# A hybrid decoder step on one core: weight loads held behind the row stores and the first gather, the decode rows turned later, and from expert 4 on the down product ahead of the next up products

## The reference, cut to what matters

```python
h  = x + merged @ w_o                        # 520 x 1024, w_o 1024 x 1024
hn = rmsnorm(h, norm2)
# hier_moe: top-1 of 4 groups, then top-2 of its 8 experts; 32 experts in all
ys = (silu(xb @ w1[e]) * (xb @ w3[e])) @ w2[e]     # w1, w3: 1024 x 512; w2: 512 x 1024
h  = h + sum over the two chosen experts of gate * ys
y  = rmsnorm(h, norm_f)
```

## Time and profile before

| | us |
|---|---|
| median of 3 runs | 1240.52 |
| the runs | 1240.52, 1242.89, 1231.26 |
| the profiled execution, its own time | 1231.87 |
| its span, first to last instruction | 1230.2 |
| PE busy in the span | 1077.6 (88%) |
| DVE, ACT, POOL busy | 348.9, 208.3, 136.8 |

### The profile page before, as it was taken

How to read it: one execution, slowest core, us unless ns; L and a number is a source line. 1 busy time by engine, 2 the same in 40 slices (tenths; PEclk the granted TensorE clock), 3 DMA queues, 4 the chain that set the end, 5 groups by cost and what they waited for, 6 DMA issues and landing times.

```text
span 1230.2 us, 16554 instructions
## 1 busy us (share of the span) xinstructions
PE 1077.6 (88%) x6863; PEld 777.5 (63%) x6863; DVE 348.9 (28%) x755; ACT 208.3 (17%) x410; POOL 136.8 (11%) x153
## 2 busy tenths in 40 slices
PE   7999999999999999999989659987787888887881
PEld 6888888888888878877845435544444444444440
DVE  4994107922322323222533411100000000000002
ACT  4103022144222222320022200000000000000002
POOL 2015300011000000000000011111111111111111
PEclk9999999999999999999999869989999999899896
DMA  6671851335465482198064568999999999999964
GB/s 220 248 264 38 296 213 50 121 99 190 180 245 213 163 330 68 35 366 336 1 258 189 213 235 329 415 412 420 416 421 419 419 419 420 422 420 416 419 276 149
DMA packets 45801, 330.96 MB, mean 269 GB/s; under 512 B 9144, under 2 KB 12296, under 8 KB 31648
## 3 DMA queue, kind: packets, MB, share of 16 engines
q1 hardware_dynamic: 31888, 258.57, 52.4%
q0 software_dynamic: 12112, 64.52, 15.0%
q10 hardware_dynamic: 1728, 6.84, 1.4%
HBM read 319.77 MB, written 62.37 MB: 311 GB/s over the span
## 4 chain that ended last, share of the span: by engine, by line
PE 63%; DMA 30%; ACT 3%; DVE 2%; issue 1%; ACTq 1%; SPq 0%; POOLq 0%; DVEq 0%
DMA arena<-in_w 25%; PE bank L822 13%; PE bank L647 13%; PE bank L1124 9%; PE bank L1006 5%; PE bank L1149 5%; PE bank L997 3%; DMA arena<-in_w_stream 2%; PE bank L660 1%; DMA hn_dram<-arena 1%; PE bank L737 1%; PE bank L918 1%; PE bank L811 1%; PE bank L837 1%; PE bank L858 1%
## 5 line engine op out<-in xcount | busy, mean ns | idle before, releaser
L1124 PE MATMUL bank<-arena 128*64 128x256 f32 x2048 | 267.3, 419 | 74.8 <-DMA arena<-in_w 71.2
L1124 PEld LDWEIGHTS bank<-arena 128*64 128x64 f32 x2048 | 164.2, 146 | 169.0 <-issue 59.6
L822 PE MATMUL bank<-arena 128*128 128x260 f32 x768 | 173.1, 384 | 0.0
L647 PE MATMUL bank<-arena 128*128 128x260 f32 x768 | 169.4, 383 | 0.7 <-DMA arena<-in_w_stream 0.7
L647 PEld LDWEIGHTS bank<-arena 128*128 128x128 f32 x768 | 145.7, 190 | 23.6 <-issue 1.1
L822 PEld LDWEIGHTS bank<-arena 128*128 128x128 f32 x768 | 144.1, 190 | 22.4 <-issue 1.2
L1149 PE MATMUL bank<-arena 128*64 128x512 f32 x512 | 115.4, 592 | 1.0 <-DVE arena L1924 1.0
L1918 DVE TENSOR_TENSOR arena<-arena,bank 128x256 f32<-128x256 f32 x32 | 13.5, 421 | 331.2 <-ACT arena L1410 331.2
L603 POOL DMA_INDIRECT y_dram<-arena,scatter_rows x32 | 50.2, 1569 | 402.1 <-ACT arena L1420 157.9
L1149 PEld LDWEIGHTS bank<-arena 128*64 128x64 f32 x512 | 37.1, 136 | 60.7 <-issue 54.3
L1410 ACT ACTIVATE arena<-bank 128x256 f32<-128x256 f32 x32 | 12.3, 384 | 365.5 <-PE bank L1124 365.5
(11 more groups left out here) (324 smaller groups left out, 1043.5 us busy)
## 6 DMA issues: line engine op xcount, KB each, us to landing
arena<-in_w SPq DMA_DIRECT2D x96, 2048.0 KB, 36.9
arena<-in_w_stream SPq DMA_DIRECT2D x56, 512.0 KB, 3.5
out_sample_swa_k<-in_cache_swa_k POOLq DMA_DIRECT2D x8, 2047.0 KB, 9.9
out_sample_swa_v<-in_cache_swa_v POOLq DMA_DIRECT2D x8, 2047.0 KB, 8.6
arena<-in_cache_mem_v SPq DMA_DIRECT2D x8, 512.0 KB, 7.7
arena<-in_w_o SPq DMA_DIRECT2D x2, 2048.0 KB, 11.3
out_sample_swa_k<-in_cache_swa_k POOLq DMA_DIRECT2D x8, 511.0 KB, 5.7
out_sample_swa_v<-in_cache_swa_v POOLq DMA_DIRECT2D x8, 511.0 KB, 5.4
```

The lines of the kernel that those rows point to most:

```text
L647: last = pe.matmul(bank[:, 2 * u + h, 0:HALF], ring[u][:, k, :], x[:, k, h * HALF:(h + 1) * HALF], start=k == 0, stop=k == KT - 1)
L822: last = pe.matmul(bank[:, h, 0:HALF], ring[n % 2][:, k, :], xn[:, k, h * HALF:(h + 1) * HALF], start=k == 0, stop=k == KT - 1)
L1124: last = pe.matmul(bank[64 * q:64 * q + CAP, 2 + u, part * FE // 2:(part + 1) * FE // 2], xgT[e // 2 % 2][:, k, 64 * u:64 * u + CAP], w[:, ...
```

## The change

Five edits, all of order:

1. SP issues n6 as before. n7 now waits for all `hn_dram` stores (`hnst`).
2. n8 and n9 wait besides for the `y_dram` stores, the last turn, and the first gather's landing (`xg` 16).
3. On PE the first turn of the decode rows stands behind the first quarter of the next group's product, and not ahead of it; the second turn, the router and the first turn of group 1 move by a quarter or less too. For i from 2 on the order is as it was.
4. On PE from expert 4 on (`LATE = 4`) `down(e-1)` stands ahead of `up(e)`. `turn_x` and `turn_hidden(e)` follow `up(e)`.
5. On ACT `y_out(e-1)` stands ahead of `silu(e)` in the same experts.

```diff
@@ SP @@
             sp.wait_ge(s["wo_mm"], 2 * NT - 1)
-            for n in range(6, NHOME - 1):
-                load_weight(n // 3, n % 3)
+            load_weight(2, 0)
+            for i in range(2):
+                sp.wait_ge(hnst[i], 16 * len(range(i, NT, 2)))
+            load_weight(2, 1)
             for i in range(3):
                 sp.wait_ge(hacc[i], 16 * len(range(i, NT, 3)))
-            for i in range(2):
-                sp.wait_ge(hnst[i], 16 * len(range(i, NT, 2)))
             sp.wait_ge(s["ht"], 2 * NT)
+            sp.wait_ge(s["xg"], 16)
+            load_weight(2, 2)
             load_weight(3, 0)
@@ PE, output rows @@
+            out_rows(1, 0)
             turn_half(0, 0)
-            for i in range(1, NT):
+            out_rows(1, 1)
+            turn_half(0, 1)
+            out_rows(1, 2)
+            pe.wait_ge(s["fold"], 1)
+            router(0)
+            turn_half(1, 0)
+            out_rows(1, 3)
+            rank(0)
+            for i in range(2, NT):
                 out_rows(i, 0)
                 turn_half(i - 1, 1)
                 out_rows(i, 1)
-                if i == 1:
-                    pe.wait_ge(s["fold"], 1)
                 router(i - 1)
                 out_rows(i, 2)
                 turn_half(i, 0)
-                if i > 1:
-                    slot_tokens(i - 2)
+                slot_tokens(i - 2)
                 out_rows(i, 3)
                 rank(i - 1)
@@ PE, experts @@
-                for e in range(NE - 1):
+                for e in range(LATE):
                     up(e)
...
                     turn_hidden(e)
-                down(NE - 2)
-                up(NE - 1)
-                turn_hidden(NE - 1)
+                for e in range(LATE, NE):
+                    down(e - 1)
+                    up(e)
+                    if e % 2 == 0 and e + 2 < NE:
+                        turn_x(e // 2 + 1)
+                    turn_hidden(e)
                 down(NE - 1)
@@ ACT, experts @@
-                for e in range(NE - 1):
+                for e in range(LATE):
                     silu(e)
                     if e > 0:
                         y_out(e - 1)
-                y_out(NE - 2)
-                silu(NE - 1)
+                for e in range(LATE, NE):
+                    y_out(e - 1)
+                    silu(e)
                 y_out(NE - 1)
```

More of the change, by code:

```diff
@@ L92 @@
 NYS = 4
+LATE = 4
 CONSTS = (("ident", P), ("triu", P), ("ones", P), ("smask", CH), ("esel", NB), ("rev4", NGRP),
```

## The result

The changed kernel takes 1230.44 us (median of 20 runs, 1226.06 to 1237.57) against 1243.22 for the kernel before (20 runs, 1231.26 to 1250.39). The ratio is 0.9904, 95% interval 0.9888 to 0.9920: 11.9 us, just inside the 1% that counts as no change here. Where a gain is given in us beside a ratio it is the ratio's (1% is 12.4 us); the difference of two medians can be up to 2 us away from it.

What follows compares the result with a forecast made beforehand. Saturated weight DMA bounds the kernel, its start hanging on `down(0)` and PE's first turn of gathered rows. Terms 2.7 + 10.3 + 0 + 0 = 13.0 us off the median 1240.52 gave 1227.5, range 1213 to 1239.

Steps and rivals of the forecast that it cites:

- What bounds the end: Full DMA stretch from n12's issue: the end moves with PE's first turn of gathered rows, 13.0 us earlier, bounds 9 and 16.
- Edit 3: Decode rows on PE: a quarter of group 1 covers the 2.68 us wait; gain 2.7 us, bounds 1.5 and 2.9.
- Edits 1 and 2: Last `hn` store and first gather: fewer loads ahead, gather 6.5 us and held by the row numbers; gain 10.3 us.
- rival A: Store and gather: store lands at 702 to 703, gather takes 8 us again; gain about 9, time 1231.5; chance 0.25.
- n6 to n11 in time: Loads ahead of n12: through by about 731.5, before n12's issue at 734.2; idle must stay under 7 us.
- Edits 4 and 5: Experts from 4 on: PE's pace of 12.8 us an expert stays hidden behind the DMA's 16.1; gain 0.
- The tail: Last expert: `up(31)` waits for the last weights, so the earlier `down(29)` gains 0, bounds 0 and 3.4 us.
- B: Store and gather: store lands at 696.9, gather takes 4.1 us; gain 17, time 1223.5; chance 0.12.
- C: Loads n8 to n11: still moving when n12 is released, full stretch starts later; gain 6, time 1234.5; chance 0.10.
- D: Experts from 4 on: PE spends more time at its lower clock and falls behind the DMA; time 1262.5; chance 0.05.
- The profiled execution: Whole span of the execution shown before: 1231.9 less 13.0 gives 1218.9 us; a spread of 1231 to 1243 expected again.

## Why the prediction was right or wrong

The total was right, 13.0 forecast and 11.9 to 12.8 measured, and the time 1227.5 against 1230.44. Of the forecast's own chance two thirds lay on faster (0.32) and one third on the same (0.16); it came out as the same, by a hair. Two of its terms were not right.

- **What bounds the end.** Right: the end moves with the first turn. In 11 of the 14 traces the way from the first turn to the last down product is 479.9 to 482.5 us; the other three have an early n12 (477.4 and 477.6) or four loads held (486.7).
- **Edit 3, 2.7 us with bounds 1.5 and 2.9.** Mis-sized. The pair of traces gives 2.5 (78.2 to 75.7), as worked out; where the clock falls it is 5.6 (83.0 with edits 1 and 2 alone, 77.4 with edit 3 added). The working took the kernel before's trace, where the clock stayed up, for the rule, and gave no bound for the clock although PE idled twice there. The quarter at half clock (6.54 against 3.63) is most of the difference. The waits allowed for `turn_half(1, 0)` and `rank(0)` came to some 0.3 (a turn of 0.58 and a rank of 0.27 in place of 0.44 and 0.14).
- **Edits 1 and 2, 10.3 us.** Too high; the steps went as in rival A. The store was to land 4.3 us after its issue and took 7.97. The engines had only n6 and two stores to move, but the first 8 us moved 2.5 MB (700 to 708 us, 318 GB/s), no more than n6 and most of one store, so the `hn` store ended behind all of it. The gather was to take 6.5 and took 7.88: it was released by the store and not by the row numbers (there in the trace after at 709.3, the store at 710.9), so it started 0.9 us behind n7, as close as the gather in the kernel before was behind n9 (0.7), and not with n7 half through. From the issue of the last store to the first turn it is 24.1 to 25.8 us with the old loads and 16.9 to 17.5 with the new ones, 8.1 on the mean: 6.7 from the store (14.9 to 8.3) and 1.4 from the gather (9.4 to 8.0). The times of edits 1 and 2 alone gave 4.5, with 8.1 just inside the interval, and those of edits 1 to 3 less edit 3 gave 8.2; why the first is so low is open.
- **n6 to n11 in time.** Right: the engines were through with them about 2.5 us ahead of n12's issue (226 GB/s from 743 to 744 us, 33 and less up to 746.5), where the working in detail had 2.7 (731.5 against 734.2). Its 7 us of slack were what the waits were allowed to leave idle, and they used most of it.
- **Edits 4 and 5, 0 us.** Right, shown by the run with them alone (1.0010) and the one without them (0.9900). The tail too: `up(31)` waited for w3 until 1195.8, as worked out ("n94 lands near 1195").
- **The rivals.** A had the mechanism of the stores right, and its 1231.5 is 1 us from the median (but its gain of 9 is 3 short, since the median that it starts from was 2.7 below that of the 20 runs). That the forecast's sum is met is luck in part: an edit 3 that was too small and edits 1 and 2 that were too large cancel. B didn't happen: the gather took 7.88 and not 4.1. C didn't happen but was produced by holding all four loads. D didn't: the clock rose.
- **The profiled execution.** 1218.9 was forecast for an execution like the one shown, 1232.27 came. The spread of 9 us ahead of the decode rows was covered only by the sentence on the spread.

## What to carry to other kernels

Where a stage is full of loads, look for what starts it, not for what stands in it: here one store, one gather and one release decided 480 us of saturated DMA behind them. Ahead of a small transfer on the critical path leave the queue empty until it has landed; but what is held goes out together and meets the next small one. A semaphore raised behind a DMA in the program is no proof that the DMA is ahead in the queue: read from the trace which of the two moved bytes first. And one trace of a kernel whose engine idles near a change of clock is one draw: take a second before a row's duration goes into a sum.

## What the runs showed of the hardware that I had not expected

- The first pair's gather (0.37 MB in the trace with n7 held and `LATE = 1`) landed in 4.3 to 4.5 us with no weight load in flight, in 7.9 to 8.0 with n7 issued 0.9 us ahead, in 8.8 with n7 issued 0.2 us ahead, and in 11.2 with three loads. With nothing in flight its first bytes moved 1.8 us after its issue; with n7 ahead of it not before 4.2 us.
- A semaphore that POOL raises behind an indirect DMA released SP 0.2 us before the record of that DMA began (708.58 and 708.77).
- Behind idles of 2.4 and 2.7 us the granted clock fell to 0.50 in some executions and not in others: the same 64 records took 3.64 to 3.68 or 5.33 to 5.36 us, the same 8 records 3.63 or 6.54 to 6.70. It fell under the 64 records in just the six traces in which it had also fallen between 545 and 560 us.
- With down ahead of up from expert 4 on PE's waits for weights are shorter (the longest of an up product 2.2 us against 4.4), and the granted clock in the full stretch is 0.99 in place of 0.94. It bought no time (ratio 1.0010): the engines moved 411 to 416 GB/s either way.
- What stays open: with the old order of the loads and n9 issued 0.7 us ahead the gather took 8.04 us in one trace and 9.73, 9.78, 9.92 and 10.02 in four others, and no run tells what decides it.
